# Whole-array products of ones in TensorE's waits, and Fourier features ahead of the scan's last outputs, in a two-block hybrid layer

## The reference, cut to what matters

```python
h = rmsnorm(x, norm1_w); proj = h @ w_in
y_a = dilated_attention(...)     # 6 heads, three dilations
y_b = gla(...)                   # chunked gated linear attention: a scan
y_c = moba_attention(...)        # 6 heads
x = x + concat([y_a, y_b, y_c]) @ w_out
h2 = rmsnorm(x, norm2_w)
x = x + square(relu(h2 @ w_ff1)) @ w_ff2
```

```python
hx = rmsnorm_2(x) * (1 + sc_a) + sh_a; ux = hx @ w_in[l]
fx = fourier_mix(...)            # fft over features and tokens, then @ w_four
ax, ac = attention_group(...)    # 8 query heads, 2 key heads
rx, rc = hgrn_group(...)         # forward and backward gated scan
x = x + g_a * (concat([fx, ax, rx]) @ w_out[l])
x = x + g_f * swiglu(rmsnorm_2(x) * (1 + sc_f) + sh_f, w_gate[l], w_up[l], w_down[l])
```

## Time and profile before

| | us |
|---|---|
| median of 3 runs | 2574.23 |
| lowest, highest of them | 2568.95, 2745.06 |
| the profiled execution | 2582.34 |
| its span, first to last instruction | 2580.6 |
| TensorE, VectorE, ScalarE, GpSimd busy | 2409.3, 1035.7, 777.5, 802.8 |

### The profile page before, as it was taken

One profiled execution on the slowest core, in us unless ns is written; L12 is line 12 of the kernel. 1 busy time (PEld: TensorE's weight loads), 2 busy tenths in 40 slices (PEclk: granted clock), 3 DMA queues, 4 the chain that ended last, 5 costly groups with the idle time before them and its releaser, 6 DMA issues.

```text
span 2580.6 us, 35232 instructions
## 1 busy us (share of the span) xinstructions
PE 2409.3 (93%) x15254; PEld 1839.2 (71%) x15254; DVE 1035.7 (40%) x1475; ACT 777.5 (30%) x953; POOL 802.8 (31%) x279
## 2 busy tenths in 40 slices
PE   7987899999999999889899999999799989899998
PEld 5763367777887883458788888888487446688886
DVE  7654446255255426622523323312452743311113
ACT  4322233123234314423311121112433533322222
POOL 3322243333442214302222222222222413343432
PEclk9985699999999998889999999999899879999999
DMA  6530034443222101012023322311211003222221
GB/s 217 187 123 18 17 138 156 163 163 116 98 73 92 42 1 48 2 51 74 33 98 115 115 98 83 146 54 37 92 41 48 2 2 114 82 98 98 98 90 57
DMA packets 36411, 218.11 MB, mean 85 GB/s; under 512 B 4152, under 2 KB 7016, under 8 KB 13088
## 3 DMA queue, kind: packets, MB, share of 16 engines
q1 hardware_dynamic: 32968, 209.44, 22.5%
q10 hardware_dynamic: 3288, 6.41, 0.7%
HBM read 213.70 MB, written 2.14 MB: 84 GB/s over the span
## 4 chain that ended last, share of the span: by engine, by line
PE 77%; DVE 6%; ACT 3%; issue 1%; POOL 1%; DMA 0%; DVEq 0%; ACTq 0%; POOLq 0%
PE PS L739 61%; PE PS L1228 2%; PE PS L1255 2%; PE PS L754 2%; DVE s_states L1635 1%; DVE a_lo L661 1%; DVE tmp L668 1%; PE PS L1940 1%; PE PS L1832 1%; PE PS L1272 1%; PE PS L2053 1%; PE PS L1240 1%; PE PS L849 1%; ACT w_hi L917 1%; DVE x L681 1%
## 5 line engine op out<-in xcount | busy, mean ns | idle before, releaser
L2189 POOL TENSOR_TENSOR w_lo<-raw,w_hi 128x2048 fp32r<-128x2048 f32 (+3 forms) x163 | 666.0, 4091 | 1464.0 <-ACT w_hi L917 1464.0
L739 PE MATMUL PS<-a_hi,w_hi 128*128 128x512 f32 (+1 forms) x2104 | 695.0, 372 | 45.3 <-DVE a_lo L661 25.3
L739 PE MATMUL PS<-a_lo,w_hi 128*128 128x512 f32 (+1 forms) x2104 | 685.3, 367 | 0.0
L739 PE MATMUL PS<-a_hi,w_lo 128*128 128x512 f32 (+1 forms) x2104 | 683.3, 366 | 0.0
L739 PEld LDWEIGHTS PS<-a_hi,w_hi 128*128 128x128 f32 x2104 | 367.6, 191 | 130.4 <-issue 54.5
L739 PEld LDWEIGHTS PS<-a_hi,w_lo 128*128 128x128 f32 x2104 | 365.1, 191 | 66.7
L739 PEld LDWEIGHTS PS<-a_lo,w_hi 128*128 128x128 f32 x2104 | 364.4, 191 | 63.3 <-issue 1.7
L917 ACT ACTIVATE w_hi<-raw 128x2048 fp32r<-128x2048 f32 (+1 forms) x145 | 270.3, 1864 | 324.3 <-PE PS L739 114.6
L739 PE MATMUL PS<-hid_hi,w_hi 128*128 128x512 f32 (+1 forms) x784 | 259.3, 367 | 1.6 <-issue 1.6
L739 PE MATMUL PS<-hid_hi,w_lo 128*128 128x512 f32 (+1 forms) x784 | 258.9, 366 | 0.0
L739 PE MATMUL PS<-hid_lo,w_hi 128*128 128x512 f32 (+1 forms) x784 | 258.4, 366 | 0.0
(11 more groups left out here) (228 smaller groups left out, 2339.7 us busy)
## 6 DMA issues: line engine op xcount, KB each, us to landing
raw<-in_w_ada SPq DMA_DIRECT2D x48, 1024.0 KB, 6.8
raw<-in_w_ff SPq DMA_DIRECT2D x32, 1024.0 KB, 4.9
raw<-in_w_in SPq DMA_DIRECT2D x22, 1024.0 KB, 4.9
raw<-in_w_gate SPq DMA_DIRECT2D x22, 1024.0 KB, 4.9
raw<-in_w_up SPq DMA_DIRECT2D x22, 1024.0 KB, 5.0
raw<-in_w_down SPq DMA_DIRECT2D x16, 1024.0 KB, 4.8
raw<-in_w_out SPq DMA_DIRECT2D x12, 1024.0 KB, 5.0
raw<-in_w_down SPq DMA_DIRECT2D x8, 768.0 KB, 4.2
```

The costliest lines, as they stand in the source:

```text
L739: mm = p.matmul(ps[:, dst], wv[:, k, idx * P:(idx + 1) * P], av[:, k, dst], start=first, stop=last)
L2189: pool.tensor_tensor(low[:, ks, :], whole[:, ks, :], high[:, ks, :].bitcast(F32), ALU.subtract).then_inc(tell.sem, 1)
```

## The change

A helper issues n products of a 128x128 matrix of ones with itself, repeated to 512 columns, into a PSUM region whose content is not needed: the first job's slot of a gemm phase, the bank of the next scores, or the bank of the sums. In a gemm they stand behind the waits for `w_lo` and the slots and ahead of the wait for the first `a_lo`. In the first attention 20 stand ahead of the first unit, 2 ahead of each unit from the second group on, behind its wait for the bank (40 units), and 4 in each of the last three steps. The Fourier part of a layer gets positions just above 0.8 for its features, and the last group's weighting on VectorE comes one tick earlier.

```diff
+        FILL_BEHIND = {"in1": 7, "out1": 11, "ff1_0": 13, "ff2_0_0": 15, "in2_1": 15, "out2_0": 11, "out2_1": 11, "ff2_1_0": 15}
+
+        def keep_busy(p, ps, n):
+            for _ in range(n):
+                p.matmul(ps[:, 0:SEQ], ones_r[:], ones_r[:].unsqueeze(1).to_broadcast([P, SEQ // P, P]), start=True, stop=True)
...
                 if rising is not None and name.startswith("out"):
                     for n in job_of[i]:
                         slot_free(n)
+                    keep_busy(p, slot(job_of[i][0]), FILL_BEHIND[name])
...
                     for n in job_of[i]:
                         slot_free(n)
+                    keep_busy(p, slot(job_of[i][0]), FILL_BEHIND.get(name, 0))
...
                 ps = scores_ps(plan, u)
+                if u >= plan["end_unit"][0]:
+                    keep_busy(p, ps, 2)
...
+            if causal:
+                keep_busy(p, scores_ps(plan, 0), 20)
             for u in plan["units_at"][0]:
                 scores(u)
...
+                    if causal and steps[s][0] == len(groups) - 1 and not steps[s][2]:
+                        bank_free(("sum", len(groups) - 1))
+                        keep_busy(p, sums_ps(plan, 0), 4)
...
-                late = 1 if causal else 3
-                if s >= late and s - late < len(steps) and steps[s - late][3]:
+                late = 1 if causal else 2 if s > len(steps) else 3
+                if s >= late and s - late < len(steps) and steps[s - late][3] and not (s - late == len(steps) - 1 and late == 3):
...
         def four_pos(k):
+            if k < NT:
+                return ATT_SHARE + 0.001 * (k + 1)
             return ATT_SHARE + (1.0 - ATT_SHARE) * (k + 1) / FOUR_TICKS
```

## The result

The changed kernel takes 2583.7 us in the median of 19 runs, the kernel before 2574.2: a ratio of 1.0032, with a 95% interval from 1.0020 to 1.0045. One execution of each, at 3031 and 2745 us, was a slow one and is left out of the ratio, which goes by all the others and not by the medians. The changed kernel is 8 us slower, where 13 us less had been forecast: its median lies at the very end of the range that had been given (2536 to 2584), and on the other side of no change. The profiled execution of the changed kernel took 2575.7 us, span 2573.9, the shortest of its runs. The profiled one of before lies 8 us above its median, so the two spans alone would show a gain.

A forecast was written before the change was run, and what follows sets the result against it. TensorE, at clock 0.55, was taken to bound the first attention. Terms -11 + 0 + 2.4 - 0.9 + 0.6 - 0.5 - 3.5 = -12.9 took the profiled 2582.3 to 2569.4 us; forecast median 2561, range 2536 to 2584.

The forecast's parts named there:

- The clock is lifted: First attention: added products raise TensorE's granted clock clearly above 0.55, and the stage gets some 11 us shorter.
- rival 1: First attention, units of groups 1 to 5: the clock is not lifted, added products only cost time; 2607 us, chance 0.13.
- What the clock gives: First attention: a group takes 15.0 us at full clock against 23.7 at half, a gain of 8.7 before added products.
- 8 units with 2 products each: First attention, per group: added products stand behind the unit's wait for the maximum and push later TensorE work by 3.7 us.
- 16 x 0.23 = 3.7: First attention: price in us of a group's added products at 0.23 each, leaving a net gain of 5.0 per group.
- Idle in waits: First attention, a group's first step: 7.0 us taken at full clock instead of 6.2, as part is waits for other engines.
- Where the clock falls: First attention: the clock falls again behind each of the three scan pieces, some 2.3 us each time until products lift it.
- term of +7: First attention: cost in us of the clock falling behind the three scan pieces, range 0 to 15.
- Gemms behind a norm: in1, ff1_0, ff2_0_0, in2_1, ff2_1_0: VectorE sets the first panel's end, so added products gain 0 us (-4 to +2).
- Gemms behind a mixed stage: Added products wait for `w_lo`: out1 +2.4 us, out2_0 -0.9, out2_1 +0.6.
- Fourier features: Moved features fill waits but leave bare waits before the means: layer 1 -0.5 us, layer 2 -3.5.
- rival 3: Fourier part's bare wait and later loads give all back, and clock relapses eat the attention's gain: 2574 us, chance 0.10.

## Why the prediction was wrong, point by point

- **The clock is lifted** (right). 0.55 became 0.81 over the earlier trace rows; rival 1, which needed it near 0.5, fell. TensorE's busy share went down meanwhile, from 98.24 to 94.39 of 117.4 us (84% to 80%), so the busy share alone doesn't tell the clock.
- **What the clock gives** (right in size). The working has 11 us net and 21 us of added products in the stage, so 32 gross; the kernel's own products became 28.6 to 31.7 us shorter.
- **"8 units with 2 products each", "16 x 0.23 = 3.7"** (wrong: this step failed). The price of an added product was taken from a row inside a gemm, where products follow one another. Here each pair stands alone among products with other weights, and it pays an entry: 0.64 us at full clock, 1.02 at half, where 0.46 and 0.86 had been taken. The 40 pairs (one of them across a change of the clock, 0.62) and three fours take 32 x 0.64 + 7 x 1.02 + 0.6 + 3.8 = 32 us from start to start instead of 21 (35 by busy time, 39.97 less some 4.8 for the first 20). That is 11 to 14 of the 18 us between -11 and +7. At the same clock of 1.00 the fifth group shows it however the overlap is counted: 3.6 us for 12 products, not 2.8.
- **Idle in waits** (too low). The waits that a faster TensorE leaves grew by 3.5 us; beyond 0.8 us in a group's first step the account had no term for them in this stage.
- **Where the clock falls** (right in part). It was to fall behind the scan pieces; the 2.3 us that each fall was to cost stand in no row. In the changed kernel's profile it falls six times between 190 and 330 us: at 246.7 in a wait of the scan and at 287.6 behind a scan piece, but also at 212.5 in a wait of 1.84 us for ScalarE behind a group's sums, at 325.2 behind another such wait, at 270.6 just ahead of a third, and at 226.2 behind a wait of 2.2 us for VectorE's maximum. So the second step in the rows above ran at half clock (7.4 us). The term of +7 happened to hold what the falls outside the scan cost: that the gain came out near the forecast is luck in this part.
- **Gemms behind a norm** (right): 0, as ff1_0 shows. ff2_1, whose first phase has 15 products, takes 349.2 or 349.3 us from its first `w_lo` to its last in all twenty profiles, with and without them.
- **Gemms behind a mixed stage** (right in sign, and in size but for out2_1). Out1, from the end of GpSimd's first `w_lo` to its last product, takes 52.6 to 54.0 us in the nine profiles with the products and 49.8 to 51.5 in the eleven without: +2.7 in the means (forecast 2.4). Out2_0, from its first `w_lo` to that of ff2_0_0, takes 84.3 or 84.4 us with them and 86.2 to 86.4 in the three profiles of before; but in five others without them, whose gemm ran at the faster of two paces (last section), it takes 85.0 to 85.2, so the products themselves are worth -0.8 (forecast -0.9). Out2_1, counted likewise, is 1.6 us longer in the means (59.5 to 61.1; forecast 0.6). The eight gemms' products together measured 1.0014, +4 us, with 0 inside the interval; the forecast was +2.
- **Fourier features** (not contradicted). -4 had been forecast; the part alone measured -1.5 and -5.4 us, with 95% of both between -10 and +1; the profiles show more, -5 to -7 in layer 2 alone against the forecast's -3.5. The bare waits came near the forecast (2.9 for 3.2, 2.2 for 2.2).
- **The rivals.** The result is past rival 3 (all given back, 2574) on the slow side. Its mechanism, that relapses eat the attention's gain, has a share in it; in the stage the larger share is the price, which no rival had as its own.

What is not settled: the failed step is shown for the stage, where the account gives +7 (second profile +8.5), and removing all of the attention's products does take 8 to 9 us off the total. But with the pairs alone removed the stage is as short as before and the total is not. The two profiles of the change don't hold the loss either: they took 2575.7 and 2577.8 us, less than its median and less than the mean of before's three (2579.1), since layer 2's mixed stage is 6 us or more shorter in both (182.5 against 188.3, 188.3 and 190.7). So the cause of the total stays open in part. Whether the 32 other products cost in later stages of most executions, whether the two paces of the last section go with the kernel, or how the stages meet the clock makes some of the differences of 0.3 to 0.5%, was not found out.

## What to carry to other kernels

Price an added product by the distance from its start to the next instruction's start in the place where it will stand, not by the pace inside a gemm: a lone pair cost 0.64 us where two in a row cost 0.46. A stage in which TensorE is busy 84% of the time has little room for products that only keep it busy: here some 30 us of clock cost 32 to 35 us of products (without the first 20) and 3.5 of waits, and neither one, two nor four per unit gave a gain. Where single executions differ by more than the forecast, let each part be timed by itself, more than once, before its profile is believed: the mixed stage of layer 2 alone was 180 to 191 us with the same code.

## What was not expected of the hardware

The same gemm runs at two paces, both at a granted clock of 1.00. The kernel before, in one phase of ff2 of layer 0 and later (TensorE's busy time and its products):

```profile
1300.00:1400.00 100.00, 100.00 (x568) 1.00 0.26 101
1640.00:1740.00 100.00, 100.00 (x579) 1.00 0.24 87
```

568 against 579 products in 100 us are 2% of the pace. In the first profile of before the slow pace lasts until about 1600 us, in the second until about 1390, in the change until about 1395 and in the change without the pairs through all of ff2 of layer 0, to 1810. In all twenty profiles a phase keeps one pace from end to end: a product of 512 and one of 256 columns take 0.353 us together or 0.347. Ff2_0_0 ran at the slow pace each time, ff2_0_1 and ff2_0_2 at either. So ff2 of layer 0 takes 567.4 to 567.8 us (one slow phase of three), about 571 (two) or about 575 (three). Its cause was not found, and neither the clock row nor a wait shows it. Two of before's three profiles have one slow phase, of the seventeen others two; that is too few to say whether the pace goes with the kernel, and it is worth up to 7 of the 8 us in question.

And the products with zeros as their moving operand lifted the clock as those with ones did: granted 0.79 from 171.5 to 343 us with 30 pairs ahead of the wait, and 0.67 in the change without any pairs.
